# Gate tables of a PEER layer from one fp32 product per token in place of three bf16 products

## The reference

```python
def peer(xn, w_q, sub_keys, u, v):                       # T = 512 tokens, 8 heads, 128 keys, top 16
    q = (xt @ w_q).reshape(T, PEER_HEADS, 2, PEER_HALF)
    s = jnp.einsum('thpc,hpnc->thpn', q, sub_keys).astype(jnp.float32)
    s1, i1 = lax.top_k(s[:, :, 0], PEER_TOPK)
    s2, i2 = lax.top_k(s[:, :, 1], PEER_TOPK)
    cand = (s1[..., :, None] + s2[..., None, :]).reshape(T, PEER_HEADS, PEER_TOPK * PEER_TOPK)
    cidx = (i1[..., :, None] * PEER_N_KEYS + i2[..., None, :]).reshape(T, PEER_HEADS, PEER_TOPK * PEER_TOPK)
    top_s, top_j = lax.top_k(cand, PEER_TOPK)
    expert = jnp.take_along_axis(cidx, top_j, axis=-1)
    gate = jax.nn.softmax(top_s, axis=-1).astype(xn.dtype)
    ...
        h = jax.nn.gelu(jnp.einsum('cd,chkd->chk', xc, u[ec]), approximate=False)
        return jnp.einsum('chk,chkd->cd', gc * h, v[ec])
```

## Time and profile before

| | |
|---|---|
| median of 3 runs | 3370.5 us (3369.85 to 3378.69) |
| the profiled execution | 3374.21 us, of which the span from the first to the last instruction is 3372.1 us |
| PE busy | 3255.9 us, 97% of the span |
| DVE busy | 2592.0 us, 77% |
| ACT busy | 1621.1 us, 48% |
| mean granted clock of TensorE | 0.982 |

### The profile page before, as it was taken

The page is one execution under the profiler, slowest core; times in us unless marked ns, Lnnn a source line. Parts: engine busy times, 40 slices in busy tenths (PEclk is TensorE's granted clock), DMA queues, the critical chain, the costliest instruction groups (busy, mean ns, idle before and its releaser), DMA issues. The chain is left out here.

```text
span 3372.1 us, 50125 instructions
## 1 busy us (share of the span) xinstructions
PE 3255.9 (97%) x18534; PEld 2908.7 (86%) x18534; DVE 2592.0 (77%) x5275; ACT 1621.1 (48%) x3007; POOL 1071.0 (32%) x666
## 2 busy tenths in 40 slices
PE   7988999999999999999999998999999999999998
PEld 7867899999999888887988876899999998888886
DVE  4764898888857888886377764799888866888886
ACT  4333247676853333334354544237776763333333
POOL 2301363434313454550000001354343322545441
PEclk9988999999999999999999998999999999999999
DMA  5103358888899999994222212348887889999995
GB/s 178 52 19 105 103 171 291 290 301 280 309 322 343 407 399 391 388 398 157 71 82 70 82 45 69 132 134 288 286 311 285 290 321 329 407 405 394 393 393 200
DMA packets 324355, 833.71 MB, mean 247 GB/s; under 512 B 26000, under 2 KB 160656, under 8 KB 320016
## 3 DMA queue, kind: packets, MB, share of 16 engines
q1 hardware_dynamic: 250384, 562.04, 46.5%
q0 software_dynamic: 73728, 268.47, 21.8%
HBM read 721.30 MB, written 109.10 MB: 246 GB/s over the span
## 5 line engine op out<-in xcount | busy, mean ns | idle before, releaser
L1941 ACT ACTIVATE peer_hi<-raw 128x1024 fp32r<-128x1024 f32 x540 | 571.0, 1058 | 660.4 <-PE p_bank L1879 524.8
L2210 DVE TENSOR_TENSOR peer_lo<-raw,peer_hi 128x1024 fp32r<-128x1024 f32 x434 | 531.0, 1224 | 324.1 <-ACT peer_hi L1941 320.0
L1807 POOL DMA_INDIRECT p_grow<-in_u_rows,p_expert x256 | 335.5, 1310 | 691.5 <-DVE p_hid L2218 674.6
L1807 POOL DMA_INDIRECT p_grow<-in_v_rows,p_expert x256 | 400.2, 1563 | 397.2 <-DVE p_acc L2227 361.7
L1879 PE MATMUL p_bank<-peer_hi,p_w_hi 128*128 128x512 f32 x1500 | 462.0, 389 | 0.4 <-DVE peer_lo L2210 0.3
L1879 PE MATMUL p_bank<-peer_lo,p_w_hi 128*128 128x512 f32 x1500 | 461.8, 389 | 0.0
L1879 PE MATMUL p_bank<-peer_hi,p_w_lo 128*128 128x512 f32 x1500 | 461.8, 389 | 0.0
L1829 PE MATMUL p1r_h_ps<-h_hi,peer_hi 128*128 128x384 f32 (+1 forms) x1152 | 399.7, 347 | 15.5 <-ACT p_h_sb L1955 10.6
L1829 PE MATMUL p0r_h_ps<-h_hi,peer_hi 128*128 128x384 f32 (+1 forms) x1152 | 400.3, 347 | 13.6 <-ACT p_h_sb L1955 8.8
L1829 PE MATMUL p0r_h_ps<-h_lo,peer_hi 128*128 128x384 f32 (+1 forms) x1152 | 394.3, 342 | 0.0
L1829 PE MATMUL p0r_h_ps<-h_hi,peer_lo 128*128 128x384 f32 (+1 forms) x1152 | 394.2, 342 | 0.0
(11 more groups left out here) (372 smaller groups left out, 5821.4 us busy)
## 6 DMA issues: line engine op xcount, KB each, us to landing
raw<-in_u SPq DMA_DIRECT2D x256, 512.0 KB
raw<-in_v SPq DMA_DIRECT2D x256, 512.0 KB
hiddens<-p_h_sb SPq DMA_DIRECT2D x256, 192.0 KB
p_w_raw<-hiddens SPq DMA_DIRECT2D x64, 768.0 KB
p_g_sb<-gates SPq DMA_DIRECT2D x64, 768.0 KB
gates<-x SPq DMA_DIRECT2D x12, 2048.0 KB
raw<-in_w_b_mix SPq DMA_DIRECT2D x38, 512.0 KB
raw<-in_w_peer_q SPq DMA_DIRECT2D x32, 512.0 KB
```

What stands on the lines that cost most here:

```text
L1807: pool.indirect_dma_start(out=grow[:, g % RG, :], out_offset=None, in_=table, in_offset=bass.IndirectOffsetOnAxis(ap=expert[:, at:at + 1], ...
L1941: act.activation(hi[:, n % NH, :], raw[:, n % NR, :], ACT.Copy).then_inc(hi_ready, 1)
L2210: dve.tensor_tensor(lo[:, m % NH, :], raw[:, m % NR, :], hi[:, m % NH, :].bitcast(F32), ALU.subtract).then_inc(lo_dve, 1)
```

## The change

One fp32 matmul per token replaces the three bf16 ones. `rows` and `cols` become fp32 with the 128 keys of a token side by side. DVE writes `rows` from an fp32 iota and fp32 places; `same` stays bf16. ACT alone makes `cols`, as the product of `same` with the whole fp32 gate. The cutting of the gates into pieces, the two multiplications on DVE and the semaphores `cut`, `cols_ready` and `first_cols` go; `weighted_cols` is new. The order of the steps and the blocks at which they are issued stay.

```diff
-            rows = early.sb("rows", [P, 2, BATCH // 2, NK, 2], BF16)
+            rows = early.sb("rows", [P, 2, BATCH, NK])
             same = early.sb("same", [P, BATCH // 2, NK, 2], BF16)
-            cols = early.sb("cols", [P, 2, PIECES, BATCH // 2, NK, 2], BF16)
-            places = early.sb("places", [P, 2, SD], BF16)
-            piece0 = early.sb("piece0", [P, SD])
-            rounded = early.sb("rounded", [P, P], BF16)
-            pieces = early.sb("pieces", [P, PIECES - 1, SD], BF16)
+            cols = early.sb("cols", [P, 2, BATCH, NK])
+            row_places = early.sb("row_places", [P, SD])
+            col_places = early.sb("col_places", [P, SD], BF16)
+            gates = early.sb("gates", [P, SD])
...
                 def place_gates(k):
                     pe.wait_ge(rows_ready, k + 1)
-                    pe.wait_ge(cols_ready, (k + 1) * (PIECES - 1))
-                    pe.wait_ge(first_cols, k + 1)
+                    pe.wait_ge(weighted_cols, k + 1)
...
-                        for c in range(PIECES):
-                            mm = pe.matmul(gate_ps[:, q % 2, v % GROUP, :], rows[:, k % 2, v // 2, :, v % 2],
-                                           cols[:, k % 2, c, v // 2, :, v % 2], start=c == 0, stop=c == PIECES - 1)
+                        mm = pe.matmul(gate_ps[:, q % 2, v % GROUP, :], rows[:, k % 2, v, :], cols[:, k % 2, v, :],
+                                       start=True, stop=True)
                         mm.then_inc(multiplied, 1)
...
-                        ins = act.activation(cols[:, k % 2, 0, v // 2, :, v % 2], same[:, v // 2, :, v % 2], ACT.Copy,
-                                             scale=piece0[:, at:at + 1])
-                    ins.then_inc(first_cols, 1)
+                        ins = act.activation(cols[:, k % 2, v, :], same[:, v // 2, :, v % 2], ACT.Copy,
+                                             scale=gates[:, at:at + 1])
+                    ins.then_inc(weighted_cols, 1)
...
-                    at, gates = slice((t - 1) * P, t * P), t_ps[:, 2 * P:3 * P]
-                    before = (t - 1) * 5
-                    if t > 1:
-
-                        dve.wait_ge(cut, before)
-                    dve.tensor_copy(rounded[:, :], gates).then_inc(cut, 1)
-                    dve.tensor_copy(places[:, :, at], t_ps[:, 0:2 * P].rearrange("p (a b) -> p a b", b=P))\
-                        .then_inc(cut, 1)
-                    dve.wait_ge(cut, before + 2)
-                    dve.tensor_copy(piece0[:, at], rounded[:, :]).then_inc(cut, 1)
-                    dve.tensor_tensor(left[:, :], gates, rounded[:, :], ALU.subtract).then_inc(cut, 1)
-                    dve.wait_ge(cut, before + 4)
-                    dve.tensor_copy(pieces[:, 0, at], left[:, :]).then_inc(cut, 1)
-                    dve.wait_ge(cut, before + 5)
-                    dve.tensor_tensor(pieces[:, 1, at], left[:, :], pieces[:, 0, at],
-                                      ALU.subtract).then_inc(done, 1)
+                    at = slice((t - 1) * P, t * P)
+                    dve.tensor_copy(row_places[:, at], t_ps[:, 0:P])
+                    dve.tensor_copy(col_places[:, at], t_ps[:, P:2 * P])
+                    dve.tensor_copy(gates[:, at], t_ps[:, 2 * P:3 * P]).then_inc(done, 1)
...
-                    dve.tensor_tensor(rows[:, k % 2, :, :, :], iota, per_token(places, 0, k),
+                    dve.tensor_tensor(rows[:, k % 2, :, :], iota_row.unsqueeze(1).broadcast_to([P, BATCH, NK]),
+                                      row_places[:, mine].unsqueeze(2).broadcast_to([P, BATCH, NK]),
                                       ALU.is_equal).then_inc(rows_ready, 1)
-                    dve.wait_ge(equal, k + 1)
-                    for c in range(PIECES - 1):
-                        dve.tensor_tensor(cols[:, k % 2, c + 1, :, :, :], same[:, :, :, :], per_token(pieces, c, k),
-                                          ALU.mult).then_inc(cols_ready, 1)
```

More of the change, by code:

```diff
@@ L1539, with peer_stage @@
 NTD = SD // TB
-def peer_stage(nc, name, ident, iota16, iota2, h, ring, src, x, rstd, rows_of, drams, final=None, next_w=None):
+def peer_stage(nc, name, ident, iota_row, iota16, iota2, h, ring, src, x, rstd, rows_of, drams, final=None, next_w=None):
     BATCH = 8
     GROUP = 4
-    PIECES = 3
     TILE_BATCHES = P // BATCH
@@ L1659, in peer_stage @@
             idle = early.sb("idle", [P, 1])
-            left = index_f
             gate_ps = early.ps("gate_ps", [P, 2, GROUP, NK])
@@ L1689, in peer_stage @@
         (hi_ready, lo_pool, lo_dve, summed, taken, keys_loaded, scored, listed, own, shift_done, exped, routed, turned,
-         cut, done, equal, rows_ready, cols_ready, multiplied, g_moved, weighted, w_hi_ready, w_lo_ready, x_loaded,
-         xrow_ready, indexed, used, hidden, weighed, added, gain_loaded, x_stored, first_cols) = [st.sem(s) for s in (
+         done, equal, rows_ready, multiplied, g_moved, weighted, w_hi_ready, w_lo_ready, x_loaded,
+         xrow_ready, indexed, used, hidden, weighed, added, gain_loaded, x_stored, weighted_cols) = [st.sem(s) for s in (
              "hi_ready", "lo_pool", "lo_dve", "summed", "taken", "keys_loaded", "scored", "listed", "own", "shift_done",
-             "exped", "routed", "turned", "cut", "done", "equal", "rows_ready", "cols_ready", "multiplied", "g_moved",
+             "exped", "routed", "turned", "done", "equal", "rows_ready", "multiplied", "g_moved",
              "weighted", "w_hi_ready", "w_lo_ready", "x_loaded", "xrow_ready", "indexed", "used", "hidden", "weighed",
-             "added", "gain_loaded", "x_stored", "first_cols")]
+             "added", "gain_loaded", "x_stored", "weighted_cols")]
         def block_source(n):
@@ L2165, in cut_gates @@
                     dve.wait_ge(turned, t)
[L2166 to L2181 removed]
+                    at = slice((t - 1) * P, t * P)
+                    dve.tensor_copy(row_places[:, at], t_ps[:, 0:P])
+                    dve.tensor_copy(col_places[:, at], t_ps[:, P:2 * P])
+                    dve.tensor_copy(gates[:, at], t_ps[:, 2 * P:3 * P]).then_inc(done, 1)
                 wide = [P, BATCH // 2, NK, 2]
                 iota = iota2[:, :, :].unsqueeze(1).broadcast_to(wide)
[L2186 to L2188 removed]
                 def one_hots(k):
+                    mine = slice(k * BATCH, (k + 1) * BATCH)
                     if k % TILE_BATCHES == 0:
@@ L2193, in one_hots @@
                     if k:
-                        dve.wait_ge(cols_ready, k * (PIECES - 1))
-                        dve.wait_ge(first_cols, k)
-                    dve.tensor_tensor(same[:, :, :, :], iota, per_token(places, 1, k), ALU.is_equal).then_inc(equal, 1)
+                        dve.wait_ge(weighted_cols, k)
+                    dve.tensor_tensor(same[:, :, :, :], iota,
+                                      col_places[:, mine].rearrange("p (a b) -> p a b", b=2).unsqueeze(2).broadcast_to(wide),
+                                      ALU.is_equal).then_inc(equal, 1)
                     if k >= 2:
                         dve.wait_ge(multiplied, (k - 1) * BATCH)
-                    dve.tensor_tensor(rows[:, k % 2, :, :, :], iota, per_token(places, 0, k),
+                    dve.tensor_tensor(rows[:, k % 2, :, :], iota_row.unsqueeze(1).broadcast_to([P, BATCH, NK]),
+                                      row_places[:, mine].unsqueeze(2).broadcast_to([P, BATCH, NK]),
                                       ALU.is_equal).then_inc(rows_ready, 1)
-                    dve.wait_ge(equal, k + 1)
-                    for c in range(PIECES - 1):
-                        dve.tensor_tensor(cols[:, k % 2, c + 1, :, :, :], same[:, :, :, :], per_token(pieces, c, k),
-                                          ALU.mult).then_inc(cols_ready, 1)
                 def lower(m):
@@ L2370, in peer @@
             src = (a[f"w_peer_q{layer}"], a[f"keys{layer}"], a[f"u{layer}"], a[f"v{layer}"])
-            peer_stage(nc, f"p{layer}", ident, iota_row[:, 0:TOPK], iota2, h, ring, src, x, rstd,
+            peer_stage(nc, f"p{layer}", ident, iota_row[:, :], iota_row[:, 0:TOPK], iota2, h, ring, src, x, rstd,
                        (a[f"u_rows{layer}"], a[f"v_rows{layer}"], a[f"ffn{layer}"].broadcast_to([P, D])), (g_dram, h_dram, x_dram),
```

3 lines of the change are left out of this document (removed).

## The result

The changed kernel took 3411.3 us in the median (3399.6 to 3416.0, 4 runs), the kernel before 3370.4: a ratio of 1.011, 95% interval 1.008 to 1.014. It is slower by 27 to 47 us, where +29.5 was forecast, and the time lies inside the range.

What follows compares the result with a forecast made beforehand. PE was taken to bound the gate stretches. Span 3372.1 + 31 (PE's batches) - 1.5 (waits between tiles) = 3401.6 us; with 2.1 around the span 3403.7, less 3.7 to the median, 3400.0; range 3381 to 3413.

Steps and rivals of the forecast that it cites:

- The main term: PE's gate batches: eight fp32 products cost 1.78 us against 1.46 for 24 bf16 ones, +31 us for 96 batches, exposed.
- the first-to-next-start difference: Low end for PE's gate batch, counting only up to the next product's start: +0.23 us a batch, +22 us.
- The weights: Rival in PE's gate batches: weight loads of 192 ns no longer hidden, +155 us, 3524; chance 0.03 together with another engine.
- The comparison's 1.22 us: DVE's row table: the fp32 comparison takes 1.22 us in place of 0.686, +0.54 a batch, hidden under PE.
- the rest, 0.7 us: PE's waits between tiles for DVE's peer_lo: part comes back in both layers, -1.5 us, between 0 and -9.3.
- Hidden: Rival: PE's term at +22 and its idle time near tile boundaries regained, within 0.3%, 3380 at the edge; chance 0.08.
- faster: Rival in PE's gate batches: fp32 records run at bf16 pitch, 0.98 us a batch, -46 us, 3324; chance 0.05.
- an engine other than PE as the bound: Rival in the gate stretches: ACT or DVE becomes the bound, needing 15 us more of ACT per 110; chance 0.03 with weights.
- The array's rival: In PE's gate batches: each fp32 product costs four bf16 ones, 1.95 us a batch, +47 us, 3416; chance 0.06.

Runs made afterwards that it cites:

- The doubled products: The changed kernel with each fp32 gate product issued twice, accumulated: 3571.8 us, 165 over the changed kernel run beside it.
- DVE's relief alone: The kernel before without DVE's two multiplications per batch, PE keeping its 24 bf16 products: 3380.1 us, 1.0016 of the kernel before.
- the repeat: The changed kernel run once more with no edit: 3406.4 us, 1.0096 of the kernel before.

## Why the prediction was right

**PE's batch.** The main term was +0.32 us a batch, from 1.46 to 1.78. The chain after shows +0.33, and 16 new records take the predicted 1.78. The price came from an operation of the same kind in another stage, with the changeovers counted; the first-to-next-start difference alone would have given +22. In the two gate stretches the profile has +15.5 and +18.8, where 48 x 0.32 = 15.4 each was foretold; 2.8 of the 18.8 are the clock. The doubled products (+165) show that the batch's time is exposed whole.

**The reason behind the price** was half seen. The weights were kept as a rival only in the form that loads of 0.192 us follow each other unhidden (3524), and against it stood that they lie beside the products. They do, and still set the pace, at 0.112; the moving columns would allow 0.109. The rule of four passes for true fp32 (the Trainium skill, "FP8 and Floating Point Precision", section TensorE Precision Notes) fits the 0.109, nearly twice the 0.057 of a bf16 record, for each of two records, but no run here separates passes from anything else that grows with the columns.

**DVE and ACT.** The comparison's 1.22 us was right, and ACT's copy came out at -0.04. DVE's total fell by 62 us, not 80. With records that overlap counted once, the work of the batches (`one_hots`) fell by 63, that of `cut_gates` by 5 and that of `use_row` by 9, while the routing grew by 16. So the batches gave less than 0.84 us each, as 96 records of 0.687 us are only 61.9 us of busy time in the earlier trace rows, and the routing took some of it back.

**The step that failed** is the -1.5 us for "the rest, 0.7 us, and its like in layer 1 can come back, since DVE enters the routing without two multiplications". They did not. The waits for peer_lo grew by 3.2 and 2.7 us, where they were to stay within 2; those behind p_h_sb shrank by 2.9 and 4.7; PE's idle time in the two gate stretches came out the same within half a microsecond; and a wait of 2.9 us brought 2.8 us of low clock with it. The step has about +3 us in place of -1.5. DVE's relief alone made the kernel 2 to 9 us slower. What was missing in that step is POOL: an operation of DVE that meets one of POOL's subtractions is held to its end, so the routing's length hangs on how the two fall together, and 155 us became 162 when DVE's timing moved. The records show it for the whole difference: the routing's held operations went from 22 to 25 and 26 a layer and their excess from 45 to 52 and 54 us, each overlapping a subtraction of POOL, and the rest stayed at 118 to 120. Adding subtractions on POOL lengthened the routing again (162 to 167 and 170). A kernel without them was not run. The wait on PE's side is then a matter of which comes last, the store of h, a low part or the routing.

**The sizes.** The forecast of +29.5 lies 11 under the first medians and 2 under the repeat. Of the span's 35.8 us, 31 are the term and 2.8 the clock in layer 1's gate stretch. The rest is 0.5 there and shifts of 1 to 2 us outside the gate tables, where the change has no work. The 2.2 us before the first key score go with a granted clock of 0.60 in place of 0.70 over 56 us; what moved the other two stays open. Some of the agreement is luck: the first median, 3411.3, lies just under the range's upper end, 3413, and one of its four runs, 3416.0, above it.

**Rivals.** Hidden, faster, and an engine other than PE as the bound were all absent: the first tile's stretch of 100 us from 540 on has PE busy for 100.00, and ACT for 82.31. The array's rival can't be told from the forecast by the time alone, since its 3416 is nearer to the first median than 3400.0 is. The batch decides: that rival needs 1.95 us, and it took 1.78.

## What to carry to other kernels

Price a product by its records as the trace has them, not by how many products there are: one fp32 product leaves two records, each as dear here as nearly two bf16 ones, so three bf16 pieces are cheaper than one fp32 product, and two pieces or one fp32r product are cheaper still (-32 us each) where the accuracy allows. For small products look at the weight loads and the moving columns as two limits, and ask which is the larger. Relief on an engine off the path can lose time, if its operations then meet those of another that hold them up: look for single operations far over their usual length and for what runs beside them.

## What the runs showed of the hardware

- fp32 weight loads of 128 columns last 192 ns and follow each other at 0.112 us; of 64 columns 138 ns and, with 64 moving columns, 0.058. bf16 loads of 128 columns last 97 ns.
- An fp32r product of 128 by 128 keeps a pace of 0.112 us, twice the 0.057 of the bf16 one, though it is a single record.
- Weights of 64 columns among products of 128 cost 0.25 us of idle time ahead of a group, which groups of the full size do not show.
- Operations of DVE that start under a 2.4 us subtraction of POOL can end only after it: 2.45 us in place of 0.28, 3.41 in place of 1.23. In the routing 22 to 26 of a layer's 442 are so held in the two kernels, for about 2.1 us each.
- While PE stood still for 2.9 us in layer 1 the granted clock fell, to 0.57 over 8 us, and the lower level cost 2.8 us. A wait of 2.8 us in layer 0 left it at 1.00, so one such wait doesn't always do it.
